# Attention probabilities times 64 value columns in two column groups, with their sums on GpSimd

## What is computed

```python
def attend(q, keys, vals, scale):
    s = jnp.einsum('bqhgd,bkhd->bhgqk', q, keys) * scale
    p = jax.nn.softmax(s.astype(jnp.float32), axis=-1).astype(vals.dtype)
    return jnp.einsum('bhgqk,bkhe->bqhge', p, vals)
```

## Time and profile before

| | us |
|---|---|
| runs (3): median, lowest, highest | 1058.33, 1055.46, 1059.82 |
| the profiled execution, its own time | 1060.43 |
| its span, first to last instruction | 1058.5 |
| TensorE busy in the span | 965.3 |
| VectorE, ScalarE, GpSimd busy | 504.3, 419.8, 136.2 |
| mean granted TensorE clock, share of full speed | 0.965 |

### The profile page before, as it was taken

How to read it: one execution, slowest core, us unless ns; L and a number is a source line. 1 busy time by engine, 2 the same in 40 slices (tenths; PEclk the granted TensorE clock), 3 DMA queues, 4 the chain that set the end, 5 groups by cost and what they waited for, 6 DMA issues and landing times.

```text
span 1058.5 us, 12485 instructions
## 1 busy us (share of the span) xinstructions
PE 965.3 (91%) x4563; PEld 669.5 (63%) x4563; DVE 504.3 (48%) x857; ACT 419.8 (40%) x750; POOL 136.2 (13%) x156
## 2 busy tenths in 40 slices
PE   1679999999899999999899969999998999999896
PEld 0368889888555554455568758789774545445475
DVE  0356334433674444554543276434548445555443
ACT  3435234321212445566760255333321244555802
POOL 3000000000243001000361010000003300100620
PEclk9889999999898999999999979999998899999999
DMA  9902121320400223122034102130413000022021
GB/s 334 279 21 60 24 77 40 80 61 2 159 1 1 80 80 102 57 79 81 1 139 97 72 20 68 52 97 4 120 32 148 1 1 1 0 80 80 1 100 79
DMA packets 71962, 74.36 MB, mean 70 GB/s; under 512 B 8196, under 2 KB 51552, under 8 KB 71776
## 3 DMA queue, kind: packets, MB, share of 16 engines
q1 hardware_dynamic: 67888, 60.81, 18.5%
q0 software_dynamic: 4016, 12.77, 3.4%
HBM read 69.37 MB, written 4.19 MB: 70 GB/s over the span
## 4 chain that ended last, share of the span: by engine, by line
PE 81%; DVE 7%; issue 3%; ACT 3%; DMA 3%; POOL 1%; SPq 1%; ACTq 0%; DVEq 0%; POOLq 0%
PE pv L1563 10%; PE bank L1395 9%; PE bank L1396 9%; PE bank L1397 9%; PE bank L1614 5%; PE bank L1524 3%; PE bank L1645 3%; PE bank L1646 3%; PE bank L1647 3%; DMA W<-in_w_mod 3%; PE bank L1491 2%; PE bank L1471 2%; PE bank L1540 2%; PE bank L1340 2%; PE bank L1383 2%
## 5 line engine op out<-in xcount | busy, mean ns | idle before, releaser
L1395 PE MATMUL bank<-hA_parts,W_parts 128*128 128x512 f32 (+1 forms) x496 | 181.1, 365 | 15.1 <-DVE W_parts L945 15.1
L1396 PE MATMUL bank<-hA_parts,W_parts 128*128 128x512 f32 (+1 forms) x496 | 175.2, 353 | 0.0
L827 ACT ACTIVATE hA<-bank 128x512 f32<-128x512 f32 (+1 forms) x168 | 92.6, 561 | 82.0 <-PE bank L1614 56.1
L1194 DVE TENSOR_REDUCE mxp<-bank 128x1 f32<-128x384 f32 x192 | 96.5, 550 | 47.3 <-PE bank L1524 47.0
L1395 PEld LDWEIGHTS bank<-hA_parts,W_parts 128*128 128x128 f32 x496 | 96.4, 194 | 31.5 <-DVE W_parts L945 15.6
L1397 PE MATMUL bank<-h_low_parts,W_parts 128*128 128x512 f32 (+1 forms) x310 | 109.9, 354 | 0.0
L1396 PEld LDWEIGHTS bank<-hA_parts,W_parts 128*128 128x128 f32 x496 | 96.3, 194 | 13.6 <-issue 2.4
L1563 PE MATMUL pv<-hA,vg 128*128 128x512 f32 (+1 forms) x168 | 83.0, 576 | 6.9 <-ACT hA L827 6.4
L1563 PE MATMUL pv<-hA,XA 128*128 128x512 f32 (+1 forms) x168 | 81.0, 563 | 2.4 <-ACT hA L827 2.3
L945 DVE TENSOR_TENSOR W_parts<-W,W_parts 128x1024 fp32r<-128x1024 f32 x44 | 53.4, 1222 | 35.7 <-ACT W_parts L597 35.6
L1212 DVE SCALAR_TENSOR_TENSOR hA<-pv,hA 64x512 f32<-64x512 f32 (+1 forms) x36 | 21.6, 599 | 91.8 <-ACT hA L770 91.6
(11 more groups left out here) (236 smaller groups left out, 1827.2 us busy)
## 6 DMA issues: line engine op xcount, KB each, us to landing
W<-in_w_mod SPq DMA_DIRECT2D x12, 2048.0 KB, 8.1
W<-in_w_in SPq DMA_DIRECT2D x42, 512.0 KB, 4.0
W<-in_w_out SPq DMA_DIRECT2D x4, 2048.0 KB, 7.9
XA<-in_x SPq DMA_DIRECT2D x4, 512.0 KB, 10.0
XA<-in_x POOLq DMA_DIRECT2D x4, 512.0 KB, 7.0
x_between_layers<-XA POOLq DMA_DIRECT2D x4, 512.0 KB, 2.9
...
```

The costliest lines, as they stand in the source:

```text
L827: act.activation(prob[slot % 4][:, 0:nq], ps("sc", l, h, q0, kt)[:, 0:nq], ACT.Exp, scale=MLA_SCALE if h < MLA_H else GQA_SCALE)\
L1194: dve.tensor_reduce(mxp[:, t, half:half + 1], ps("mx", l, h, q0, t, half)[:, 0:384], AX, ALU.max).then_inc(*up("part_max", l, h, q0, t, half))
L1395: pe.matmul(p[:, 0:c[1]], high[:, k, :], h_hi[:, k, toks], start=(k == 0), stop=False)
L1396: pe.matmul(p[:, 0:c[1]], low[:, k, :], h_hi[:, k, toks], start=False, stop=False)
```

## The change

**pv.** The value operand has 64 columns, without ones. The queries of a unit are cut in two halves, and each half is a product of its own with the same 64 columns: the first half's result goes to rows 0 to 63 of the bank, the second's to rows 64 to 127. There are six `prob` buffers instead of four (`PROBS`).

**Sums.** GpSimd adds up the probability tiles of a head (`prob_sums`: five additions of 128x512 for the latent queries, one of 128x256 for the context). TensorE multiplies the total by 64 columns of ones, again in two halves (`den`, into a ring bank). `den` of a head's latent queries stands behind the first score of the next head, that of the context queries behind unit 3. `recip` waits for `den`. It and `normalise` now work on half the columns: `recip` with 128 rows, `normalise` in two instructions.

**GQA without pads.** `maxes` takes 64 rows, line 1620's product (now 1658) takes 65, and the row of maxima moves from 96 to 64. The memsets of the pads go.

**w_out.** The eight pieces of block 0 are rounded one at a time in heads 8, 9 and 10 (`W_HIGH_AT`), and GpSimd subtracts five after the sums of head 9 and three after those of head 10; block 1 is done wholly behind the last `y_high`.

The additions of probabilities (lines 510 and 515) stand in the queue between what was there, and the 16 subtractions are cut into five, three and eight. The diff, cut:

```diff
+PROBS = 6
+W_HIGH_AT = [(8, 5), (9, 1), (9, 2), (9, 3), (9, 4), (10, 1), (10, 2), (10, 3)]
...
-        prob = [hA[:, 3072 + 512 * i:3584 + 512 * i] for i in range(4)]
-        rd, un = hA[:, 5120:5632], hA[:, 5632:6144]
+        rd, un = hA[:, 5120:5376], hA[:, 5632:6144]
...
-        vm = XA[:, 0:3456].rearrange("p (t r c) -> p t r c", t=TILES, r=3)
+        vm = XA[:, 0:2304].rearrange("p (t h v) -> p t h v", t=TILES, h=MLA_H)
...
-        vg = sb("vg", [P, TILES, 2, 192])
+        vg = sb("vg", [P, TILES, 2, 64])
+        last_sum = sb("last_sum", [P, 512])
...
+        spare = h_low_f32[:].rearrange("p k t -> p (k t)")[:, 3 * T:5 * T].rearrange("p (i n) -> p i n", i=3)
+        prob = [hA[:, 3072 + 512 * i:3584 + 512 * i] for i in range(4)] + [spare[:, i, :] for i in range(2)]
+        psum = [spare[:, 2, :], last_sum[:]]
         q_both, q_high = ([y_hi[:, (2 * i + o) * T:(2 * i + o + 1) * T] for i in range(2)] for o in range(2))
-        k_twice, k_low = ([e[:].rearrange("p f h c -> p (f h c)")[:, o * T:(o + 1) * T]
-                           for e in (wuq_parts, wukv_parts)] for o in range(2))
+        k_twice = [e[:].rearrange("p f h c -> p (f h c)")[:, 0:T] for e in (wuq_parts, wukv_parts)]
+        k_low = [h_low[:, 1 + g, :] for g in range(2)]
...
-        w_hi = [pieces(gqk_parts[:].rearrange("p f t -> p (f t)"), glav_parts[:].rearrange("p t c -> p (t c)")),
-                pieces(rounded[:].rearrange("p f t -> p (f t)"), glaqk_parts[:].rearrange("p f t -> p (f t)"),
-                       sq_parts[:].rearrange("p a b -> p (a b)"))]
+        w_hi = [pieces(glav_parts[:].rearrange("p t c -> p (t c)"), glaqk_parts[:].rearrange("p f t -> p (f t)"),
+                       sq_parts[:].rearrange("p a b -> p (a b)")),
+                pieces(gqk_parts[:].rearrange("p f t -> p (f t)"), rounded[:].rearrange("p f t -> p (f t)"))]
...
+        def summed(l, slot):
+
+            per = sum(nk // P for _, _, nk in qbs(l))
+            u = slot % per
+            return slot + 1 if u == 0 or (l < DEPTH - 1 and u == 2) else slot
...
-                for h in heads[1:MLA_H]:
-                    round_k(l, h)
-
...
+                def prob_sums(h, q0, nq, nk):
+
+                    i = pv_index(l, h, q0)
+                    total = psum[i % 2][:, 0:nq]
+                    first = slot_of(l, h, q0)
+                    if i >= 2:
+                        pool.wait_ge(*at("filled", "den", *pv_owner(i - 2)))
+                    pool.wait_ge(*at("prob", l, first + 1))
+                    pool.tensor_tensor(total, prob[first % PROBS][:, 0:nq], prob[(first + 1) % PROBS][:, 0:nq],
+                                       ALU.add).then_inc(*up("prob_sum", l, first + 1))
+                    for sl in range(first + 2, first + nk // P):
+                        pool.wait_ge(*at("prob", l, sl))
+                        pool.wait_ge(*at("prob_sum", l, sl - 1))
+                        pool.tensor_tensor(total, total, prob[sl % PROBS][:, 0:nq], ALU.add)\
+                            .then_inc(*up("prob_sum", l, sl))
+                    pool.wait_ge(*at("prob_sum", l, first + nk // P - 1))
+
+                def weights_low(n, ks):
                     i = W_POS[("out", l, n)]
-                    for k in range(KD):
+                    for k in ks:
                         pool.wait_ge(*at("w_hi", l, n, k))
                         pool.tensor_tensor(w_lo[:, i % 2, k, :], W[:, i % 2, k, :], w_hi[n][k].bitcast(F32),
                                            ALU.subtract).then_inc(*up("w_lo", l, n, k))
...
+                for h in heads:
+                    if len(qbs(l)) == 2:
+                        prob_sums(h, *qbs(l)[0])
+                    if h + 1 < MLA_H:
+                        round_k(l, h + 1)
+                    if h == MLA_H + 1:
...
+                    if h + 1 < MLA_H:
+                        pool.wait_ge(*at("round_k", l, h + 1))
+                    prob_sums(h, *qbs(l)[-1])
+                    if h == heads[-3]:
+                        weights_low(0, range(5))
+                        pool.wait_ge(*at("w_lo", l, 0, 4))
+                    if h == heads[-2]:
+                        weights_low(0, range(5, KD))
+                        pool.wait_ge(*at("w_lo", l, 0, KD - 1))
+                weights_low(1, range(KD))
...
-                    pv = pv_banks[pv_index(l, h, q0) % 2]
-                    r, s = 64 * (h % 2), 64 - 64 * (h % 2)
-                    act.wait_ge(*at("pv_filled", l, h, q0))
+                    n2 = nq // 2
+                    act.wait_ge(*at("filled", "den", l, h, q0))
                     if recips:
                         act.wait_ge(*at("o_scaled", *recips[-1]))
-                    act.activation(rd[r:r + 64, 0:nq], pv[s:s + 64, 0:nq], ACT.Ln).then_inc(*up("den_ln", l, h, q0))
+                    act.activation(rd[:, 0:n2], ps("den", l, h, q0)[:, 0:n2], ACT.Ln).then_inc(*up("den_ln", l, h, q0))
+                    let_go(("den", l, h, q0), "den_ln", l, h, q0)
                     act.wait_ge(*at("den_ln", l, h, q0))
-                    act.activation(rd[r:r + 64, 0:nq], rd[r:r + 64, 0:nq], ACT.Exp, scale=-1.0)\
-                        .then_inc(*up("recip", l, h, q0))
+                    act.activation(rd[:, 0:n2], rd[:, 0:n2], ACT.Exp, scale=-1.0).then_inc(*up("recip", l, h, q0))
...
-                        queries = (qh if h < MLA_H else q_high)[h % 2]
-                        act.activation(queries[96:97, q0:q0 + nq], ps("nm", l, h, q0)[0:1, 0:nq], ACT.Copy)\
+                        queries = qh[h % 2][96:97, :] if h < MLA_H else q_high[h % 2][64:65, :]
+                        act.activation(queries[:, q0:q0 + nq], ps("nm", l, h, q0)[0:1, 0:nq], ACT.Copy)\
...
-                        if slot >= 4:
-                            act.wait_ge(*at(*prob_reader(l, slot - 4)))
-                        act.activation(prob[slot % 4][:, 0:nq], ps("sc", l, h, q0, kt)[:, 0:nq], ACT.Exp,
+                        if slot >= PROBS:
+                            act.wait_ge(*at(*prob_reader(l, slot - PROBS)))
+                            act.wait_ge(*at("prob_sum", l, summed(l, slot - PROBS)))
+                        act.activation(prob[slot % PROBS][:, 0:nq], ps("sc", l, h, q0, kt)[:, 0:nq], ACT.Exp,
...
-                        c = j - 3 if h == heads[-2] else j + len(todo) - 4 if h == heads[-1] and j else -1
-                        if 0 <= c < KD:
-                            w_high(2 * c // KD, (2 * c % KD, 2 * c % KD + 1))
+                        u = j - len(todo) + TILES
+                        if h in (8, 9, 10) and (h, u) in W_HIGH_AT:
+                            w_high(0, (W_HIGH_AT.index((h, u)),))
...
+                w_high(1, range(KD))
...
-                        src = ps("vp", l, t)[:, 0:384].rearrange("p (r e v) -> p r e v", r=3, e=2)
-                        for e in range(2):
-                            dve.tensor_copy(vm[:, t, :, 128 * e:128 * e + 64], src[:, :, e, :])\
-                                .then_inc(*up("vm", l, t, e))
-                        let_go(("vp", l, t), "vm", l, t, 1)
+                        dve.tensor_copy(vm[:, t, :, :], ps("vp", l, t)[:, 0:384].rearrange("p (h v) -> p h v", h=MLA_H))\
+                            .then_inc(*up("vm", l, t))
+                        let_go(("vp", l, t), "vm", l, t)
...
-                    r, s = 64 * (h % 2), 64 - 64 * (h % 2)
+                    r, n2 = 64 * (h % 2), nq // 2
...
-                    dve.scalar_tensor_tensor(out=un[r:r + 64, 0:nq], in0=pv[r:r + 64, 0:nq], scalar=0.5,
-                                             in1=rd[r:r + 64, 0:nq], op0=ALU.mult, op1=ALU.mult)\
-                        .then_inc(*up("o_scaled", l, h, q0))
+                    for e in range(2):
+                        half = slice(64 * e, 64 * e + 64)
+                        dve.scalar_tensor_tensor(out=un[r:r + 64, n2 * e:n2 * e + n2], in0=pv[half, 0:n2], scalar=0.5,
+                                                 in1=rd[half, 0:n2], op0=ALU.mult, op1=ALU.mult)\
+                            .then_inc(*up("o_scaled", l, h, q0))
...
-                            pe.wait_ge(*at("q_pad", l, h % 2))
-                            q, k = q_high[h % 2][0:96, :], k_twice[(h - MLA_H) // 3][0:96, :]
+                            q, k = q_high[h % 2][0:64, :], k_twice[(h - MLA_H) // 3][0:64, :]
...
-                    e = h % 2
-                    if h < MLA_H:
-                        v = vm[:, kt, h // 2, 64 * e:64 * e + P]
-                    else:
-                        v = vg[:, kt, (h - MLA_H) // 3, 64 * e:64 * e + P]
+                    v = vm[:, kt, h, :] if h < MLA_H else vg[:, kt, (h - MLA_H) // 3, :]
                     if h == 0 and kt == 0:
-                        pe.wait_ge(*at("vm", l, TILES - 1, 1))
-                        pe.wait_ge(*at("vg", l, TILES - 1, 1))
-                    mm = pe.matmul(pv_banks[i % 2][:, 0:nq], v, prob[sl % 4][:, 0:nq], start=(kt == 0),
```

(23 more changed lines are left out.)

60 lines of the change are left out of this document (24 added, 36 removed).

## The result

The changed kernel takes 1109.1 us (median of 4 runs, 1103.9 to 1113.4), the kernel before 1059.1 beside it: a ratio of 1.047, 95% interval 1.042 to 1.052, some 50 us slower. Ratios and means, here and in the experiments, leave out a run more than 1.5% above the fastest of its kernel, which is one of e2's four (1109.2 us). The direction was forecast, the size was not: 1076 us, with a range up to 1092. The profiled execution took 1103.9 us (span 1101.6), 43.5 more than that of before. I read first the page's busy shares and its clock row, then the busy times of the heads' stretches in both kernels.

What follows compares the result with a forecast made beforehand. The prediction took TensorE's work to bound the heads. TensorE +21.5, w_out waits -5, exp waits -2 and -1, GpSimd waits +4 gave +17.5 on 1058.3, or 1076 us; range 1058 to 1092.

Steps and rivals of the forecast that it cites:

- Shape changes, +72.9: TensorE: 468 array shape changes instead of 56, each costing empty time and mostly exposed load; +72.9 us.
- the forecast's -3 for the earlier exps: TensorE's exp waits before pv: -2 us for shape changes hidden under them, -1 for exps earlier through shorter recip.
- +21.5: TensorE's sum in us: -53.9 streaming, +72.9 shape changes, +2.5 gain not had at turned maxima waiting for VectorE.
- Waits that go: TensorE's idle time at w_out's rounding, heads 10 and 11, disappears: -5 us, bounds 0 and -8.
- Waits that come, +4 (bounds +1 and +20): GpSimd's new sums make den late at three places with less cover: +4 us.
- A: Rival: shape changes cost little in TensorE's dense stream; 1000 us, or 1040 if only loads are hidden; 11%.
- D: Rival: pv's two halves do not run at once inside the heads; 1140 us; 1%.
- B: Rival: TensorE's existing waits at layer 0's head starts swallow most added gaps; 1062 us; 12%.
- C: Rival: GpSimd becomes the bound, additions of 1.74 us or more making each head's den 0.8 late; 1095 us; 7%.

Runs made afterwards that it cites:

- e2: The changed kernel with the pads of the grouped heads put back, so maxes has the full shape again; 1101.3 us, ratio to before 1.037.
- e3: The changed kernel with pads back and pv and den each one product of 128 stationary columns, without column groups; 1092.7 us, ratio to before 1.032.
- e8: The changed kernel with pv and den each one 64-column product in one half of the array, no pairs; 1135.4 us, ratio to before 1.071.
- e10: The changed kernel, pairs kept, with repeated work ahead of each score product making every unit 0.43 us longer; 1134.7 us, ratio to before 1.070.
- e6: The changed kernel with GpSimd's additions after the first of each sum cut to 8 of 512 columns; 1098.5 us, ratio to before 1.038.
- e4: The kernel before with only the changed rounding of w_out taken over; 1049.8 us, ratio to before 0.993.
- e9: As e3, but without the pads, so the grouped heads' maxes keep 64 rows; 1108.6 us, ratio to before 1.045.

## Why the prediction was right and wrong

- **The step that failed** is one that isn't in the sum: all costs were taken at the full clock, since the heads of before have 1.00 in every row. The changed stream does not hold it: 0.88 and 0.96 in the heads. 25 to 38 us, half to three quarters of the result, are missing there, and no rival had it. I had read how long the units get and not what the clock does when a unit's full products get fewer and empty time comes between them. That this thinner stream loses the clock is shown by e3, e8 and e10 against after and e6; why it stays low under a busy TensorE is open.
- **Shape changes, +72.9**: each price held (0.96 to the pair, 0.34 behind it, units of 1.99 and 1.79 against about 2.0 and 1.8). Whether their sum was too high depends on the clock's part. With e4's -7.9, e6's 11.0 for the sums and the forecast's -3 for the earlier exps, the rest's +11.7 leaves some +12 for TensorE where I had +21.5; by two thirds of "lost" it leaves +24. That not all of a lengthening shows where TensorE waits anyway, e9 (10.6 of 22.7), e8 (at most 57 of 67) and e3 (51 to 62 for 72.9) show; how much of it is in the changed kernel they don't.
- **Waits that go**: -7.9 for `w_out` by e4, forecast -5; the 2.10 wait and those before the out products of layer 1 are gone. The exp's waits fell by 7.7 us, more than the 3 that I took.
- **Waits that come, +4 (bounds +1 and +20)**: 11.0 by e6, the term that was sized too small. The additions took 1.3 us as said, but head 10 of layer 0 cost 3.29 instead of 1, since I summed 6.5 us of subtractions and set against them a cover that the context's two units don't have, and layer 1's end 5.23 instead of half of 1. What VectorE loses beside GpSimd, 687 to 1428 ns, I had weighed only for GpSimd's side.
- **The rivals**: A is refuted by the units, D by the pair's four records in two passes. B's mechanism, waits that take up added time, shows in e9 and e8, but the changed kernel is far from B's 1062. C, `den` late in most heads, is not what happened: seven waits, two of them large.
